# One inverse root on VectorE for the head norms of q and k together, instead of one for each

## The reference

```python
def rms_norm(x, g):
    xf = x.astype(jnp.float32)
    y = xf * lax.rsqrt(jnp.mean(xf * xf, axis=-1, keepdims=True) + EPS)
    return (y * g.astype(jnp.float32)).astype(x.dtype)

def mla_branch(c_q, c_kv, k_r, q_lat_g, w_uq, kv_lat_g, w_ukv, q_norm_g, k_norm_g, cos, sin):
    ...
    q = (rms_norm(c_q, q_lat_g) @ w_uq).reshape(B, S, MLA_HEADS, QK_DIM)
    kv = (rms_norm(c_kv, kv_lat_g) @ w_ukv).reshape(B, S, MLA_HEADS, QK_NOPE + V_DIM)
    ...
    k = jnp.concatenate([k_nope, k_rope], axis=-1)
    q = rms_norm(q, q_norm_g)
    k = rms_norm(k, k_norm_g)
    ...
    return causal_block_attention(q, k, v)   # scores times 1/sqrt(96), softmax
```

## Time and profile before

| | |
|---|---|
| time, median of 3 runs | 1435.34 us (1434.59 to 1435.9) |
| the profiled execution: its own time / its span | 1435.21 us / 1433.4 us |
| PE matmul busy | 1424.1 us (99% of the span) |
| DVE busy | 1143.1 us (80%), 1160 instructions |
| ACT busy | 960.6 us (67%), 1003 instructions |
| granted TensorE clock, mean | 0.999 |

### The profile page before, as it was taken

The page is one execution under the profiler, slowest core; times in us unless marked ns, Lnnn a source line. Parts: engine busy times, 40 slices in busy tenths (PEclk is TensorE's granted clock), DMA queues, the critical chain, the costliest instruction groups (busy, mean ns, idle before and its releaser), DMA issues.

```text
span 1433.4 us, 19210 instructions
## 1 busy us (share of the span) xinstructions
PE 1424.1 (99%) x6747; PEld 1178.6 (82%) x6747; DVE 1143.1 (80%) x1160; ACT 960.6 (67%) x1003; POOL 45.3 (3%) x54
## 2 busy tenths in 40 slices
PE   9999999999999999999999999999999999999998
PEld 7888778888888888778888888888888888888886
DVE  6987756665547977756989898898898988989986
ACT  6676754544435676754677787777777777777775
POOL 2000003000000000000200000000000000000200
PEclk9999999999999999999999999999999999999999
DMA  9473348955465473447899999999999999999994
GB/s 338 162 236 118 119 157 305 332 177 178 159 214 187 149 234 118 136 159 276 290 352 414 410 359 411 380 386 409 366 402 380 380 412 372 382 386 413 372 397 161
DMA packets 163268, 415.14 MB, mean 290 GB/s; under 512 B 15420, under 2 KB 43960, under 8 KB 163176
## 3 DMA queue, kind: packets, MB, share of 16 engines
q1 hardware_dynamic: 157128, 393.42, 74.7%
q0 software_dynamic: 5008, 16.97, 3.6%
q10 hardware_dynamic: 1040, 3.68, 0.6%
HBM read 398.20 MB, written 15.81 MB: 289 GB/s over the span
## 4 chain that ended last, share of the span: by engine, by line
PE 96%; ACT 2%; DVE 2%; issue 0%; POOL 0%; DVEq 0%; ACTq 0%; POOLq 0%
PE ps L552 88%; PE ps L1109 1%; PE ps L829 1%; PE ps L972 1%; PE ps L951 1%; PE ps L873 1%; PE ps L959 1%; ACT w_hi L507 1%; ACT qk_t L1252 1%; PE ps L938 0%; PE ps L907 0%; PE ps L950 0%; ACT prob L1377 0%; ACT sq L1377 0%; PE ps L846 0%
## 5 line engine op out<-in xcount | busy, mean ns | idle before, releaser
L512 DVE TENSOR_TENSOR w_lo<-raw,w_hi 128x2048 fp32r<-128x2048 f32 (+3 forms) x240 | 500.9, 2105 | 139.2 <-ACT w_hi L507 136.5
L507 ACT ACTIVATE w_hi<-raw 128x2048 fp32r<-128x2048 f32 (+3 forms) x240 | 421.9, 1769 | 187.2 <-PE ps L552 171.5
L552 PE MATMUL ps<-w_hi,act_hi 128*128 128x512 f32 (+1 forms) x1264 | 333.8, 392 | 0.1
L552 PE MATMUL ps<-w_hi,act_lo 128*128 128x512 f32 (+1 forms) x1264 | 331.3, 388 | 0.0
L552 PE MATMUL ps<-w_lo,act_hi 128*128 128x512 f32 (+1 forms) x1264 | 327.4, 387 | 0.0
L552 PEld LDWEIGHTS ps<-w_lo,act_hi 128*128 128x128 f32 x1264 | 235.6, 188 | 48.1
L552 PEld LDWEIGHTS ps<-w_hi,act_lo 128*128 128x128 f32 x1264 | 234.9, 188 | 47.8 <-DVE act_lo L1621 0.2
L552 PEld LDWEIGHTS ps<-w_hi,act_hi 128*128 128x128 f32 x1264 | 232.3, 188 | 46.0 <-ACT act_hi L1252 0.5
L512 DVE TENSOR_TENSOR w_lo<-raw_more,w_hi 128x2048 fp32r<-128x2048 f32 (+1 forms) x96 | 201.9, 2111 | 30.3 <-ACT w_hi L507 30.2
L507 ACT ACTIVATE w_hi<-raw_more 128x2048 fp32r<-128x2048 f32 (+1 forms) x96 | 170.0, 1775 | 55.4 <-PE ps L552 54.4
L512 DVE TENSOR_TENSOR w_lo<-raw_low,w_hi 128x2048 fp32r<-128x2048 f32 (+1 forms) x64 | 137.6, 2156 | 11.2 <-ACT w_hi L507 10.7
(11 more groups left out here) (285 smaller groups left out, 1232.0 us busy)
## 6 DMA issues: line engine op xcount, KB each, us to landing
raw<-in_moe_w_gu SPq DMA_DIRECT2D x128, 512.0 KB, 9.3
raw_more<-in_moe_w_down SPq DMA_DIRECT2D x80, 512.0 KB, 7.4
raw<-in_w_in SPq DMA_DIRECT2D x72, 512.0 KB, 4.7
raw_low<-in_moe_w_gu SPq DMA_DIRECT2D x64, 512.0 KB, 10.6
raw_more<-in_moe_w_gu SPq DMA_DIRECT2D x64, 512.0 KB, 10.8
raw<-in_moe_w_gu SPq DMA_DIRECT2D x64, 384.0 KB, 7.7
raw<-in_moe_w_down SPq DMA_DIRECT2D x48, 512.0 KB, 7.1
raw<-in_dense_w_gu SPq DMA_DIRECT2D x44, 512.0 KB, 5.0
```

The costliest lines, as they stand in the source:

```text
L507: nc.scalar.activation(w_hi[:, self.split_slot(j), 0:n], self.raw(j)[:, 0:n], ACT.Copy).then_inc(self.hi, 1)
L512: nc.vector.tensor_tensor(w_lo[:, c, 0:n], self.raw(j)[:, 0:n], w_hi[:, c, 0:n].bitcast(F32), ALU.subtract).then_inc(self.lo, 1)
L552: return nc.tensor.matmul(dst, a, b, start=start and n == 0, stop=stop and n == 2)
```

## The change

`q_sum` and `k_sum` become the two halves of one tile, `head_sum` (128x64). At q's second sums the root is left out. At k's second sums one root is made over all 64 columns, with q's scale and epsilon for both (`1.0`, `DQ * EPS`). k's factor thereby comes out smaller by 1/sqrt(96), and `qk_gain` is multiplied by sqrt(96) when it is made, once at the start. The three working tiles of the root become 64 columns wide.

```diff
-        rs_a = sb("rs_a", [P, TT * H])
-        rs_t = sb("rs_t", [P, TT * H])
-        rs_y = sb("rs_y", [P, TT * H], I32)
+        rs_a = sb("rs_a", [P, 2 * TT * H])
+        rs_t = sb("rs_t", [P, 2 * TT * H])
+        rs_y = sb("rs_y", [P, 2 * TT * H], I32)
...
-        q_sum = sb("q_sum", [P, TT, H], F32, mixer)
-        k_sum = sb("k_sum", [P, TT, H], F32, mixer)
+        head_sum = sb("head_sum", [P, 2, TT, H], F32, mixer)
+        q_sum, k_sum = head_sum[:, 0], head_sum[:, 1]
...
-                        nc.vector.memset(qk_gain[DN:DQ, :], 1.0)
-                        tt(qk_gain[0:DN, :], gain_q[0:DN, :], gain_k[0:DN, :], ALU.mult)
+                        nc.vector.memset(qk_gain[DN:DQ, :], 1.0 / SCALE)
+                        stt(qk_gain[0:DN, :], gain_q[0:DN, :], 1.0 / SCALE, gain_k[0:DN, :], ALU.mult, ALU.mult)
...
                     if not hf:
                         continue
+                    if step[2] == "q":
+                        continue
                     dve.wait_ge(head_sums, counts["heads"])
-                    flat = v[:].rearrange("p t h -> p (t h)")
-                    if step[2] == "q":
-
-                        root(flat, flat, 1.0, DQ * EPS, TT * H)
-                    else:
-                        link(tt(v[:], v[:], over(small[:, 12:14], H), ALU.add))
-                        root(flat, flat, 1.0 / DQ, EPS, TT * H)
+                    link(tt(v, v, over(small[:, 12:14], H), ALU.add))
+                    flat = head_sum[:].rearrange("p i t h -> p (i t h)")
+
+                    root(flat, flat, 1.0, DQ * EPS, 2 * TT * H)
```

## The result

The changed kernel takes 1439.72 us (median of 9 runs, 1437.93 to 1441.56) against 1435.59 us for the one before in the same comparison (9 runs, 1434.59 to 1435.9). The ratio is 1.0029, with a 95% interval of 1.0021 to 1.0037: 4.1 us slower. I had forecast 1435.3 us, no change. The profiled execution of the changed kernel took 1439.16 us, with a span of 1437.4 at a granted clock of 0.999.

The account below looks back on a forecast made before the run. PE was taken to bound the kernel, with DVE ahead of it at both roots. The profiled 1435.21 us, minus 0, plus 0, gave 1435.2; with the runs' median 1435.34, the forecast was 1435.3 us, range 1433.8 to 1436.9.

Parts of the forecast that it names:

- the split: DVE's 128x1024 split behind q's root in the first layer, claimed to start at about 83.1 us instead of 84.77.
- the ten steps: The common root's chain at k's sums, 64 columns: 2.5 us, about 219 to 225 ns each instruction.
- the cover: DVE's idle stretch before 106.77 us, behind k's root: swallows the longer root's 0.3 us, shrinking from 3.4 to about 3.1.
- no wait of PE between 60 and 120 us: Across the first layer's roots, PE was claimed to run products without a gap; a new wait there would show the forecast wrong.
- DVE's busy time: Over both layers, claimed to fall by 3.2 us from q's omitted root, less the wider root's extra.
- The sum for the instructions: Profiled execution of 1435.21 us, minus 0 for the removed root, plus 0 for the wider one: 1435.2.
- Rival 1: VectorE's saving at q's root shows up in full: 3.9 us in all, 1431.4 us; chance 3%.
- the wait on ACT: Behind q's root, DVE stands still from 84.3 until ACT's next part ends at 86.0 us, using up the saving.
- The rest: Remaining edits: qk_gain's product, the scale ACT applies, no step moved past a queue, no wait added; claimed to cost nothing.
- Where those 2.23 us go: Behind q's root, the time saved per layer becomes one DVE idle stretch of 1.7 us, of no use to PE.
- signs of being wrong: A new PE wait between 60 and 120 us, slower ACT copies at 83 to 88, or DVE pauses at expert-loop jumps.
- Rival 2: Expert loop's DVE code shifts and pauses at jumps back; at 4 us a pause, 5 us slower, 1440.3; chance 3%.

Follow-up runs that it names:

- the second experiment: The changed kernel with the root's working tiles at their old width, the 64-column root working in prob_t instead: 1435.16 us against 1435.16, ratio 1.0000.

## Why the prediction was wrong

**What held.** The steps in the mixer held one by one: 83.16 us for the split (about 83.1 forecast), 1.75 us idle behind it (1.7), 2.51 us for the ten steps (2.5), 3.02 us left of the cover (3.1), no wait of PE between 60 and 120 us. DVE's busy time fell from 1143.1 to 1139.2 us, 3.9 instead of 3.2; 3.1 of it lies ahead of the experts. Of the steps on 64 columns, seven take 224 to 227 ns each and three 195, where the prediction had 219 to 225 for all. The sum for the instructions was zero, and the second experiment, which has them all at the old addresses, measured zero (1.0000). Rival 1 did not come about: the wait on ACT ate the saving, as its working said.

**The step that failed** is the paragraph "The rest". It costs the edits that are not instructions of the root, and leaves one of them out altogether: the wider declarations of `rs_a`, `rs_t` and `rs_y`. I had them in the diff and costed ten instructions on 64 columns, but not the 384 bytes by which everything behind moves. In place of that nothing the runs show +3.7 us for the declarations alone (1438.86 - 1435.16) and 0 without them. They move `raw_more` off a multiple of 256 bytes, the loads fall behind, and PE waits for weight chunks in the last expert. The remark under "Where those 2.23 us go" that neither DVE nor PE waits for a transfer in these rows was true of these rows; I never asked it of the experts. None of the signs of being wrong that it lists looks at a load either. The page before the change has the transfer engines full there, in each of its 40 slices from 717 us on but the last:

```profile
DMA  9473348955465473447899999999999999999994
```

**Rival 2** had the sign and 3% for it, but the wrong mechanism. It did move its eyes to the experts, yet to the jump of a loop, and took the changed code as the only thing that lies elsewhere after such an edit. The pauses stayed, and the kernel without the 20 instructions, with the old addresses, is as fast as before.

**The range** of 1433.8 to 1436.9 was drawn from the spread of the runs and a margin for "another build", with no mechanism behind the margin. The places of tiles, which cost 4 us, are no part of it.

**What stays open.** Whether the other shifted tiles add a small part is not settled: the landings suggest it and the times can't tell. That the backlog and the gather together stop PE is shown; how near the kernel before is to that edge was not measured. Moving the last of the three slot tiles off the multiple, with a rate lower by up to 2% in the stretches shown, was enough in most runs, and a few runs showed no loss.

## What to carry to other kernels

A declaration is an edit of every tile behind it: before costing a wider working tile at nothing, look at which load destinations move, and whether they begin on a multiple of 256 bytes. Where the transfer engines are full for a whole stage, a loss of some 2% in their rate can be a cost even if the page shows PE at 99%; here it came due where another queue joined in, not where it arose. When a small edit moves the time and the trace around it agrees with the forecast, run its declarations without its instructions, and its instructions without its declarations; here these two kernels told one from the other.

## What the runs showed of the hardware

The place at which a load's rows begin in on-chip memory changes its rate: 420 GB/s at a multiple of 256 bytes, 409 to 410 at 32, 64 or 128 bytes past one, for rows of 4096 bytes on 16 full transfer engines. I had not expected that the price would be flat. The Trainium skill ("DMA: Bandwidth & Descriptors", How a descriptor splits into AXI transactions) has a descriptor cut into pieces of 256 bytes, with one more piece where its start is off a 256-byte boundary, and with bytes fetched ahead of the start that still cost beats. That a start off the boundary costs, the runs bear out, here for the destination, while the page's rule on the start speaks of reads. Worked out from the page's beats of 32 bytes, an estimate for 4096 bytes is 132 beats instead of 128 at 128 bytes past the boundary (3.1%), 130 at 64 (1.6%) and 129 at 32 (0.8%). The runs show 2.4 to 2.7% at all three, so the number of beats is not what sets it here. One more piece in each row (17 instead of 16) would be the same for all three; no run here counts the pieces.
